# Relative places in SBUF of TensorE's two operands: from constant to climbing from 0 to 64 bytes

## The reference

```
proj = einsum('bsd,de->bse', rmsnorm(x), w_in)        # 2048 x 16400
y_a  = sigmoid(o_g) * norm(mlstm(q, k, v)) * silu(z_a)
br_a, br_b = y_a @ w_proj_mlstm, y_b @ w_proj_pool
out  = (sigmoid(g_a) * br_a + sigmoid(g_b) * br_b) @ w_out
proj2 = rmsnorm_2(h) @ w_in_2                          # 2048 x 5952, 272 tokens
```

## Time and profile before

| | us |
|---|---|
| median of 3 runs (1504.67 to 1509.2) | 1508.79 |
| the profiled execution | 1507.16 |
| its span, first to last instruction | 1504.2 |
| TensorE busy | 1470.4 (98%) |
| VectorE busy | 846.3 (56%) |
| ScalarE busy | 703.5 (47%) |
| DMA, mean over the span | 176 GB/s |

### The profile page before, as it was taken

One profiled execution on the slowest core, in us unless ns is written; L12 is line 12 of the kernel. 1 busy time (PEld: TensorE's weight loads), 2 busy tenths in 40 slices (PEclk: granted clock), 3 DMA queues, 4 the chain that ended last, 5 costly groups with the idle time before them and its releaser, 6 DMA issues.

```text
span 1504.2 us, 27822 instructions
## 1 busy us (share of the span) xinstructions
PE 1470.4 (98%) x10850; PEld 1388.2 (92%) x10850; DVE 846.3 (56%) x1047; ACT 703.5 (47%) x921; POOL 63.5 (4%) x89
## 2 busy tenths in 40 slices
PE   7999999999999999999999999999999999999997
PEld 6999988899999999999999998879999988888886
DVE  5667755546646655545454545556554545556754
ACT  6544535455454433434433434446333345566542
POOL 0000000001010000000000000000000001111000
PEclk9999999999999999999999999999999999999999
DMA  7566555655456555666666667657555543333663
GB/s 280 169 194 195 170 179 169 208 158 165 154 167 183 184 164 173 184 189 186 182 186 190 181 187 266 193 166 233 173 169 164 173 154 99 99 108 104 207 210 126
DMA packets 70645, 264.79 MB, mean 176 GB/s; under 512 B 7840, under 2 KB 7840, under 8 KB 69408
## 3 DMA queue, kind: packets, MB, share of 16 engines
q1 hardware_dynamic: 69552, 254.24, 54.8%
q0 software_dynamic: 1024, 9.57, 1.7%
HBM read 259.58 MB, written 4.19 MB: 175 GB/s over the span
## 4 chain that ended last, share of the span: by engine, by line
PE 95%; DVE 2%; ACT 1%; issue 1%; DMA 0%; DVEq 0%; POOL 0%; ACTq 0%; SPq 0%; POOLq 0%
PE ps L328 23%; PE ps L332 23%; PE ps L330 23%; PE ps L318 6%; PE ps L320 6%; PE ps L319 6%; PE ps L433 2%; PE ps L677 1%; PE ps L506 1%; PE ps L514 1%; PE ps L684 1%; PE ps L682 0%; DMA xn<-in_x 0%; DVE wl L1121 0%; PE ps L538 0%
## 5 line engine op out<-in xcount | busy, mean ns | idle before, releaser
L1121 DVE TENSOR_TENSOR wl<-raw,wh 128x1024 fp32r<-128x1024 f32 x474 | 580.2, 1227 | 538.5 <-ACT wh L826 530.3
L826 ACT ACTIVATE wh<-raw 128x1024 fp32r<-128x1024 f32 x474 | 500.2, 1061 | 569.8 <-PE ps L332 441.2
L328 PE MATMUL ps<-xh,wh 128*128 128x256 f32 x1792 | 503.9, 281 | 1.0 <-DVE xl L1137 1.0
L330 PE MATMUL ps<-xl,wh 128*128 128x256 f32 x1792 | 500.3, 279 | 0.0
L332 PE MATMUL ps<-xh,wl 128*128 128x256 f32 x1792 | 499.9, 279 | 0.0
L328 PEld LDWEIGHTS ps<-xh,wh 128*128 128x128 f32 x1792 | 336.5, 188 | 1.6 <-DVE xl L1137 1.3
L330 PEld LDWEIGHTS ps<-xl,wh 128*128 128x128 f32 x1792 | 336.0, 187 | 0.3
L332 PEld LDWEIGHTS ps<-xh,wl 128*128 128x128 f32 x1792 | 336.1, 188 | 0.0
L328 PE MATMUL ps<-x2h,wh 128*128 128x256 f32 (+1 forms) x688 | 198.4, 288 | 4.0 <-DVE avt L1277 1.8
L332 PE MATMUL ps<-x2h,wl 128*128 128x256 f32 (+1 forms) x688 | 194.8, 283 | 0.0
L330 PE MATMUL ps<-x2l,wh 128*128 128x256 f32 (+1 forms) x688 | 194.5, 283 | 0.0
(11 more groups left out here) (325 smaller groups left out, 1770.8 us busy)
## 6 DMA issues: line engine op xcount, KB each, us to landing
raw<-in_w_stream SPq DMA_DIRECT2D x474, 512.0 KB, 3.7
xn<-in_x SPq DMA_DIRECT2D x2, 1024.0 KB, 6.2
xr<-in_x POOLq DMA_DIRECT2D x1, 2048.0 KB, 11.8
x_kept<-xr POOLq DMA_DIRECT2D x1, 2048.0 KB, 8.1
x1r<-x_kept POOLq DMA_DIRECT2D x1, 2048.0 KB, 11.1
out<-yn SPq DMA_DIRECT2D x4, 512.0 KB, 2.7
poolw<-in_pool_w POOLq DMA_DIRECT2D x1, 1024.0 KB, 6.5
postw<-in_post_w POOLq DMA_DIRECT2D x1, 1024.0 KB, 5.1
```

The lines of the kernel that those rows point to most:

```text
L328: pe.matmul(out_at(j), whr[:, c, f], hi[:, kc, tokens], start=st, stop=False, skip_group_check=True)
L330: pe.matmul(out_at(j), whr[:, c, f], lo[:, kc, tokens], start=False, stop=False, skip_group_check=True)
L826: act.activation(slot_view(wh_at[r], layout), raw[r][:, :, :], ACT.Copy).then_inc(wh_done, 1)
L1121: tt(slot_view(wl_at[r], layout), raw[r][:, :, :], slot_view(wh_at[r], layout).bitcast(F32), ALU.subtract).then_inc(split_done, 1)
```

## The change

The activation x (`xh`, `xl`) gets a ramp: chunk kc is moved on by 4 * min(kc, 4) words, so 0, 16, 32, 48, 64, 64, ... bytes. The weights of all groups by feature on x lie at 0 instead of 192 bytes; the relative place is then 0, 16, 32, 48 for chunks 0 to 3 and 64 for chunks 4 to 15. Weights of `v` lie at 64 bytes, so that its relative place is 192, 208, 224, 240 for chunks 0 to 3 and 0 from chunk 4. `yh` and `yl` get a pitch of 260 words, and the slots of `pa` a first place and pitch by slot with the same result: 0, 16, 32, 48, then 64. The slots of `ckv`, `ak`, `av` and `aq` likewise, where it alternated between 64 and 192: 0 and 4 words, 8 and 12, then 16, so in bytes 0, 16, 32, 48, 64 again. `wo`, `cq`, `g`, `w2`, `pb`, `uq`, `ur`, `uk` and `uv` keep their layouts, only that the first three slots of `wo` and `v` follow the new layout of the stage before. To make room for 256 bytes more in each of x's and y's two tiles, the tiles behind them move by 512 bytes and the causal mask loses its last 128 columns, which are a copy of its first ones. No instruction is added or removed, and no wait.

```diff
 SLOT_W = 1088
+RAMP = [4 * min(kc, 4) for kc in range(KC + 1)]
 BY_FEATURE, BY_TOKEN, SECOND, SECOND_KEYS = (48, 512), (0, 512), (0, 528), (16, 528)
-LAYOUT_OF = {"v": BY_TOKEN, "wo": BY_TOKEN, "uv": BY_TOKEN, "w2": BY_TOKEN, "cq": SECOND_KEYS, "ckv": SECOND_KEYS,
-             "ak": SECOND_KEYS, "av": SECOND_KEYS, "aq": SECOND, "g": SECOND}
+ON_RAMP, TOKEN_RAMP = (0, 512), (16, 512)
+LAYOUT_OF = {"qk": ON_RAMP, "o": ON_RAMP, "z": ON_RAMP, "u": ON_RAMP, "zb": ON_RAMP, "ga": ON_RAMP, "gb": ON_RAMP,
+             "v": TOKEN_RAMP, "wo": BY_TOKEN, "uv": BY_TOKEN, "w2": BY_TOKEN, "cq": SECOND_KEYS, "g": SECOND}
+
+
+def layout_of(kind, k):
+
+    if kind == "pa":
+        return (0, 512) if k < 2 else (8 * k - 16, 516)
+    if kind in ("ckv", "ak", "av"):
+        return ((0, 524), (24, 524), (48, 528), (16, 528))[k if k < 2 else 2 + k % 2]
+    if kind == "aq":
+        return ((16, 524), (40, 524), (0, 528), (32, 528))[k if k < 2 else 2 + k % 2]
+    return LAYOUT_OF.get(kind, BY_FEATURE)
 
 
 def slot_layouts():
 
-    out = []
+    out, last = [], []
     for name, kinds, times in STAGES:
-        of = [LAYOUT_OF.get(kind, BY_FEATURE) for kind in kinds for _ in range(slots_of(kind))] * times
+        of = [layout_of(kind, k) for kind in kinds for k in range(slots_of(kind))] * times
         if name in ("V", "WO"):
-            of[:LEAD] = out[-LEAD:]
+            of[:LEAD] = last[:LEAD]
         out += of
+        last = of
     return out
...
 CONST, CONST_W = packed((
-    ("ones", 128), ("dmask", 384), ("inv", 64), ("rel", KEYS),
+    ("ones", 128), ("dmask", S), ("inv", 64), ("rel", KEYS),
...
-    R_X, R_C, R_Y, R_Z, R_V, R_T = 51200, 86016, 118784, 151552, 167936, 184384
+    R_X, R_C, R_Y, R_Z, R_V, R_T = 51200, 86016, 118784, 152064, 168448, 184896
...
 
         first, pitch = layout
-        return slot[:, first:first + SLOT_KC * pitch].rearrange("p (c n) -> p c n", n=pitch)[:, :, 0:COLS]
-
-    xh = sb("xh", [P, KC, S], F32R, R_X)
-    xl = sb("xl", [P, KC, S], F32R, R_X + 16384)
+        return bass.AP(slot[:, 0:1].tensor, first, [[SLOT_W, P], [pitch, SLOT_KC], [1, COLS]])
+
+    xh = sb("xh", [P, KC * S + RAMP[KC]], F32R, R_X)
+    xl = sb("xl", [P, KC * S + RAMP[KC]], F32R, R_X + 16640)
+
+    def ramped(t):
+
+        return lambda kc: t[:, kc * S + RAMP[kc]:(kc + 1) * S + RAMP[kc]]
+
+    def plain(t):
+        return lambda kc: t[:, kc, :]
+
     qk = sb("qk", [P, 2 * KC, S], F32, R_C)
-    yh = sb("yh", [P, KC, S], F32R, R_Y)
-    yl = sb("yl", [P, KC, S], F32R, R_Y + 16384)
+    yh = sb("yh", [P, KC, S + 4], F32R, R_Y)
+    yl = sb("yl", [P, KC, S + 4], F32R, R_Y + 16640)
...
-    r1row = cn("dmask", 0, L2)
+    r1row = const[:, CONST["dmask"][0]:CONST["dmask"][0] + L2]
...
-                        pe.matmul(o, hi[:, kc, t], whr[:, c, 0:cols], start=a, stop=False)
-                        pe.matmul(o, hi[:, kc, t], wlr[:, c, 0:cols], start=False, stop=False)
-                        last = pe.matmul(o, lo[:, kc, t], whr[:, c, 0:cols], start=False, stop=z)
+                        pe.matmul(o, hi(kc)[:, t], whr[:, c, 0:cols], start=a, stop=False)
+                        pe.matmul(o, hi(kc)[:, t], wlr[:, c, 0:cols], start=False, stop=False)
+                        last = pe.matmul(o, lo(kc)[:, t], whr[:, c, 0:cols], start=False, stop=z)
...
-                        pe.matmul(out_at(j), whr[:, c, f], hi[:, kc, tokens], start=st, stop=False,
+                        pe.matmul(out_at(j), whr[:, c, f], hi(kc)[:, tokens], start=st, stop=False,
                                   skip_group_check=True)
-                        pe.matmul(out_at(j), whr[:, c, f], lo[:, kc, tokens], start=False, stop=False,
+                        pe.matmul(out_at(j), whr[:, c, f], lo(kc)[:, tokens], start=False, stop=False,
                                   skip_group_check=True)
-                        last = pe.matmul(out_at(j), wlr[:, c, f], hi[:, kc, tokens], start=False, stop=z,
+                        last = pe.matmul(out_at(j), wlr[:, c, f], hi(kc)[:, tokens], start=False, stop=z,
...
-        X, Y, Z = (xh, xl), (yh, yl), (zh, zl)
+        X, Y, Z = (ramped(xh), ramped(xl)), (plain(yh), plain(yl)), (plain(zh), plain(zl))
...
-            pe.matmul(o, wgh[:, kc, :], xh[:, kc, :], start=kc == 0, stop=False)
-            pe.matmul(o, wgl[:, kc, :], xh[:, kc, :], start=False, stop=False)
-            last = pe.matmul(o, wgh[:, kc, :], xl[:, kc, :], start=False, stop=kc == KC - 1)
+            pe.matmul(o, wgh[:, kc, :], ramped(xh)(kc), start=kc == 0, stop=False)
+            pe.matmul(o, wgl[:, kc, :], ramped(xh)(kc), start=False, stop=False)
+            last = pe.matmul(o, wgh[:, kc, :], ramped(xl)(kc), start=False, stop=kc == KC - 1)
...
-            high_parts(xh, b, "norm_pre", s_x_high)
+            high_parts(ramped(xh), b, "norm_pre", s_x_high)
...
-                    split_high_low(yh[:, bass.ds(i * 4, 4), :], yl[:, bass.ds(i * 4, 4), :], t[:, :, :], s_y)
+                    split_high_low(yh[:, bass.ds(i * 4, 4), 0:S], yl[:, bass.ds(i * 4, 4), 0:S], t[:, :, :], s_y)
...
-                            scalar=stat[:, bass.ds(h + 32 + 8 * st, 1)], in1=cn("dmask", st * S, w),
+                            scalar=stat[:, bass.ds(h + 32 + 8 * st, 1)], in1=cn("dmask", 0, w),
...
-    put("dmask", np.concatenate([seen[:P, :], seen[P:, P:]], 1))
+    put("dmask", seen[:P, :])
```

More of the change, by code:

```diff
@@ L564, in _ @@
         for i in range(2):
-            groups("WO", i, {"wo": (mh, ml)}, token_kinds=("wo",),
+            groups("WO", i, {"wo": (plain(mh), plain(ml))}, token_kinds=("wo",),
                    before=lambda j, kind, k: merged_there(i, j, k))
         uses = [FIRST_G["CKQ"] // 2, FIRST_G["CKQ"] // 2]
-        X2 = (x2h, x2l)
+        X2 = (plain(x2h), plain(x2l))
         xtok = [slice(META, META + P), slice(META + P, L2)]
@@ L647, in _ @@
         for j in range(3):
-            pe_group(pe, n, [(psum_free[j % 2], uses[j % 2], 0)], half_bank(j % 2), (cqh, cql), None, slice(0, S),
+            pe_group(pe, n, [(psum_free[j % 2], uses[j % 2], 0)], half_bank(j % 2), (plain(cqh), plain(cql)), None, slice(0, S),
                      kcs=4, ring=n % RING)
@@ L653, in _ @@
         for j in range(2):
-            pe_group(pe, n, both(), whole_bank(0, L2), (ckh, ckl), None, slice(0, L2), kcs=2, ring=n % RING)
+            pe_group(pe, n, both(), whole_bank(0, L2), (plain(ckh), plain(ckl)), None, slice(0, L2), kcs=2, ring=n % RING)
             used(0, 1)
@@ L665, in _ @@
         for j in range(2):
-            pe_group(pe, n, both(), whole_bank(0), (ckh, ckl), [slice(t * P, (t + 1) * P) for t in range(3)], None,
+            pe_group(pe, n, both(), whole_bank(0), (plain(ckh), plain(ckl)), [slice(t * P, (t + 1) * P) for t in range(3)], None,
                      kcs=2, ring=n % RING)
@@ L765, in _ @@
             pe_group(pe, FIRST["W2"] + j * GROUP, [(s_y_summed, 2 * (j - 1), 0)] if j >= 2 else [(s_gsum, 4, 0) if j else (pair["max_m"], H, 0)],
-                     whole_bank(2 * (1 - j % 2)), (oh, ol), [slice(0, P), slice(P, S)], None,
+                     whole_bank(2 * (1 - j % 2)), (plain(oh), plain(ol)), [slice(0, P), slice(P, S)], None,
                      ring=FIRST["W2"] % RING, before=out_there, first_tile_early=j == 3, chunk=lambda kc: OUT_ORDER[kc // 4] * 4 + kc % 4)
@@ L837, in high_parts @@
                 for c in (2 * p, 2 * p + 1):
-                    last = act.activation(hi[:, c, :], turned_chunk(c), ACT.Copy,
+                    last = act.activation(hi(c), turned_chunk(c), ACT.Copy,
                                           scale=sm(name, c, 1))
@@ L1076, in x2_high_parts @@
             act.wait_ge(s_x2_turned, b + 1)
-            high_parts(x2h[:, :, META:L2], b, "attn_norm", s_x2_high)
+            high_parts(plain(x2h[:, :, META:L2]), b, "attn_norm", s_x2_high)
         def between():
@@ L1136, in low_parts @@
                 for c in (2 * p, 2 * p + 1):
-                    last = stt(out=lo[:, c, :], in0=turned_chunk(c), scalar=sm(name, c, 1),
-                               in1=hi[:, c, :].bitcast(F32), op0=ALU.mult, op1=ALU.subtract)
+                    last = stt(out=lo(c), in0=turned_chunk(c), scalar=sm(name, c, 1),
+                               in1=hi(c).bitcast(F32), op0=ALU.mult, op1=ALU.subtract)
                 last.then_inc(s, 1)
         for b in range(4):
-            low_parts(xl, xh, b, "norm_pre", s_x_high, s_x_low)
+            low_parts(ramped(xl), ramped(xh), b, "norm_pre", s_x_high, s_x_low)
             if b + 1 < LEAD:
@@ L1547, in x2_low_parts @@
         def x2_low_parts(b):
-            low_parts(x2l[:, :, META:L2], x2h[:, :, META:L2], b, "attn_norm", s_x2_high, s_x2_low)
+            low_parts(plain(x2l[:, :, META:L2]), plain(x2h[:, :, META:L2]), b, "attn_norm", s_x2_high, s_x2_low)
         def between():
```

## The result

Five runs of the changed kernel took 1497.18 us in the median (1495.35 to 1497.22), five of the kernel before, beside them, 1508.03; the ratio is 0.9931, 95% interval 0.9915 to 0.9947. The change wins 0.7%, some 10 us, where 22 were forecast. The profiled execution took 1497.18 us, its span is 1495.3 (1504.2 before).

A forecast was written before the change was run, and what follows sets the result against it. TensorE, busy 98% of the span, was taken as the bound, so matmul start-to-start time counts. Quick-level gains of 22.4 less 0.2 us gave 22 us off 1507.2, so 1485, stated as 1486 for the median; range 1460 to 1518.

The forecast's parts named there:

- The two levels and their 4.5 ns: 256-column matmuls at place 64 run at 113.3 or 117.8 ns; the climb was to reach the quick level, 4.5 ns less.
- I take 113.3 as for the rest: Chunks 1 to 3 at places 16 to 48, not in the trace, charged 113.3 ns; bounds -5.3 or +14 us.
- The gate matmuls' 117 ns: 48 gate matmuls passing through many relative places take 5.62 us, 117 ns each, between the bounds for chunks 1 to 3.
- The bound from V, 124.7: Upper bound per matmul for chunks 1 to 3: 117.8 plus V's place difference of 6.9 ns.
- `pa`: 4 groups, 3.5: The four groups of `pa` were to win 3.5 us by reaching the quick level.
- OZ: Eight groups, only chunks 0 to 5 counted, win 2.6 us; later chunks, drawn anew, up to 4.3 more.
- AQ: Three of four chunks stood at 118 ns; two groups by 144 matmuls were to win 1.3 us.
- `ckv`, `ak`, `av`: 912 matmuls of 272 columns, half at 192: +1.0 us if at 126.3 ns, -1.0 if at 124.2; taken as 0.
- nearly half of its time free: VectorE and ScalarE, with nearly half their time free, were to hide DVE and ACT writes 16 bytes further on: 0 us.
- nothing happens: Rival: the jump to 0 and the small steps leave TensorE on the slow level, 1508 us; chance 0.13.
- The ramp itself is dear: Rival: 64 stays slow and chunks 0 to 3 read from colliding places, 1511 to 1523 us; chance 0.17.
- A third, quicker level: Rival: the climb arrives below 113.3 ns, at 109 for 256-column matmuls, giving 1460 us; chance 0.12.

The follow-up runs named there:

- the two constant kernels: Changed kernel without climb: x's groups held at place 64, 1506.4 us; or x and y without ramp, first-block groups by feature held at 192, 1505.7 us.
- the jump: Changed kernel with x's ramp made one jump, chunk 0 at place 0 and chunks 1 to 15 at 64: 1507.6 us.
- the last step alone: Changed kernel with only the ramp's last step, chunk 0 at place 48 and chunks 1 to 15 at 64: 1504.7 us.
- 32 to 64: Changed kernel with x climbing 32, 48, 64 only; `zb` and `gb` weights moved to other places: 1507.1 us.
- 16 to 64: Changed kernel with x climbing 16, 32, 48, 64, without the 0; `pa` climbs by its weights alone, y at its old pitch: 1505.0 us.
- the kernel with both operands moving: Changed kernel with x climbing 16 bytes every chunk and its groups' weights following from chunk 4, relative place kept; `pa` constant at 64: 1510.3 us.

## Why the prediction was off

Point by point, in the prediction's own terms:

- **The two levels and their 4.5 ns: right, and the way in a lucky pick.** 113.3 and 117.8 ns are what x's groups have, and the climb leads from one to the other. `ga`, `u` and seven of QK's eight groups are quick in chunks 4 to 15 in the profile. That constant places stay slow holds for 64 and for 192 in MG (the two constant kernels). But no row of the trace before led to the claim that this climb arrives on the quick level; I had taken it because it was the level left to reach. Of four other ways up, the jump led in nowhere, the last step alone in 6 of 27 groups, 32 to 64 in 4 of 21 and 16 to 64 in 4 of 27. So the direction was right by luck as far as my argument goes.
- **"I take 113.3 as for the rest", chunks 1 to 3: wrong, the largest miss.** The four chunks were charged 117.8 + 3 x 113.3 = 457.7 and took 119.2 + 119.4 + 116.4 + 118.3 = 473.3 ns: 15.6 x 12 = 0.19 us a group, 6.4 us in 34 groups. My reason for the value, that the steps should have the rest's price, was none. The gate matmuls' 117 ns over many places, which I had called "between", was the row to take: 4 x 117 = 468. The bound from V, 124.7, was too high: chunks 1 to 3 have 118.0 in the mean.
- **"`pa`: 4 groups, 3.5": wrong.** It arrives and loses the level at chunk 5: chunks 4 to 15 at 117.9 in the mean instead of 113.3, 4 x 144 x 4.6 = 2.7 us. I had treated the relative place as all that counts; the kernel with both operands moving shows that it is not. The earlier trace rows had said so already, and I misread them: AQ's chunk 3 keeps the place of chunk 2, 192, so no step of the place lost its quick level (1.36, then 1.41 us); what moves there is both operands, by 64 bytes.
- **OZ: the first part right, the sum wrong** (2.2 us forecast with chunk 0 taken off, 0.7 us longer measured). Chunks 4 and 5 are quick in all eight groups, the climb costs 1.5, and from chunk 6 on the level is drawn anew. But I had counted that draw as unchanged, and it came out slow in all of them: 326 quick matmuls in chunks 6 to 15 before, by their starts, 0 after, 326 x 4.5 = 1.5 us. Why the draw changed wasn't tried (the kernel with the ramp of x alone has it slow in all eight too); where a step to 192 stands behind the head's matmuls, it is quick in all eight.
- **QK's first group** is interrupted by transposes and stayed slow: 144 x 4.5 = 0.6 us.
- **AQ: mostly wrong**, 0.2 us instead of 1.2 (1.0 short, 0.4 of it by the ramp term above): the climb led in in neither group, chunk 4 is at 117.7 in both, and one found the quick level behind the transposes. It is so in all nine kernels with this layout of AQ: 117.6 to 117.7 at chunk 4 in all 18 groups. Unlike on x, both operands move there at every chunk; that this is why wasn't tried alone. **`ckv`, `ak`, `av`:** +0.7 us, near my bound of +1.0, since 64 held is 126.2 ns there as in the earlier trace rows; I had taken 0. V +0.3, WO -0.2, as said. G +0.2, UQ and W2 within 0.1.

The sum: 22.4 - 6.4 - 2.7 - 1.5 - 0.6 - 0.6 - 0.7, and 0.3 less for V, WO and G together, is 9.6 us; the stages' times differ by 9.4, the spans by 8.9, the medians by 10.9. One reading besides was off without an effect: VectorE has not nearly half of its time free in QK, it is busy for 15.53 of 22.61 us.

The rivals: *nothing happens* fell with the groups' 22.0 us. *The ramp itself is dear* had the right sign for the first four chunks, but at 0.5 ns above the slow level and not 6.9: 4 x 12 matmuls cost 0.03 us a group more than before, twelve chunks win 0.65. By the sign that I had given for it, the first four chunks above 118 ns, it was met for those chunks (118.3 in the mean), and the sign was a poor one: it says nothing of the twelve behind. *A third, quicker level* was not seen in any kernel. The Trainium skill's two independent read ports ("TensorE: Matmul & The Clock Gate", "Step-by-step: what each phase is for") don't by themselves explain what is measured here: one and the same pair of addresses runs at either rate.

## What to carry to other kernels

When a matmul stream's start-to-start time is above its quickest stretch at the same shapes, look for two levels before looking for a cost per address: cut the stream into chunks and see whether a level persists and where it changes. Then test where in a group it can be led in; a constant's measured time is no price of its place, and a short detour (here two chunks at 112 ahead of fourteen at 192) may be worth more than any constant tried. And charge an unseen state by the rows that average over many such states, not by the one hoped for.

## What the runs showed of the hardware that was not expected

- 256-column float32r matmuls with a 128x128 weight load each ran at 113.3 or 117.8 ns at places 64 and 192, and at 120.0, 118.3, 116.7 or 113.3 at 112, all at a granted clock of 1.00, and held a level for 180 matmuls and more (113.3 and 117.8 in the last step's two groups of `u`, 120.0 in QK at 112). Groups with the same addresses ran at different levels, so something ahead of them decides.
- In the kernel that climbed on by 16 bytes a chunk, groups begun at 0, 64, 128 and 192 had after a few chunks the same time at the same place, to 0.2 ns. Two such steps are not enough: from 80 by 96 to 112 `gb` stayed at 120.0.
- Both operands moving on by 16 bytes at a chunk boundary ended the quick level at once, in `pa` and on x (118.0 and 118.7 ns); moving on by 64 bytes ended it in AQ at place 192 (1.36, then 1.41 us) and not at place 64 (113.4 to 113.5 for ten chunks).
- The step from 112 to 192 led into the quick level in all uninterrupted groups of two executions, from the 120.0 and from the 118.3 ns level at 112 alike. What makes the levels stays open: the traces show starts, and no stall inside a matmul.
